# Four V tiles to a PSUM bank, gathers without staged row numbers, and U low parts ahead of the routing

## What is computed

```
q  = (h @ w_q) -> [t, 8 heads, 2, 128];  s = q . sub_keys (128 keys a half)
s1,i1 = top_k(s[:,:,0], 16);  s2,i2 = top_k(s[:,:,1], 16)
top_s,pos = top_k(s1 + s2 over all 256 pairs, 16);  idx = i1*128 + i2 at pos;  gate = softmax(top_s)
act = gelu(einsum('td,tkd->tk', x, u[idx]))          # 8*16 = 128 experts a token
out = einsum('tk,tkd->td', gate * act, v[idx])       # u, v: 16384 experts x 2048
```

## Time and profile before

| | us |
|---|---|
| median of 3 runs | 5671.56 (5666.36 to 5677.82) |
| the profiled execution | 5670.56 |
| its span, first to last instruction | 5668.8 |
| TensorE busy | 5059.5 (89%) |
| VectorE busy | 3760.8 (66%) |
| ScalarE busy | 1407.4 (25%) |
| GpSimd busy | 2950.0 (52%) |

### The profile page before, as it was taken

The page is one execution under the profiler, slowest core; times in us unless marked ns, Lnnn a source line. Parts: engine busy times, 40 slices in busy tenths (PEclk is TensorE's granted clock), DMA queues, the critical chain, the costliest instruction groups (busy, mean ns, idle before and its releaser), DMA issues. The chain is left out here.

```text
span 5668.8 us, 72848 instructions
## 1 busy us (share of the span) xinstructions
PE 5059.5 (89%) x25836; PEld 4495.4 (79%) x25836; DVE 3760.8 (66%) x5187; ACT 1407.4 (25%) x1138; POOL 2950.0 (52%) x1263
## 2 busy tenths in 40 slices
PE   6999979999998999999799899988997888888887
PEld 5877757777776787877599899988897888878786
DVE  3566658888887001001388799954327999999998
ACT  2223322222222222112232344422221111111111
POOL 2333323333332443443344555589986777777774
PEclk7999989999998999999899999999998999999999
DMA  1222212121212333333233577777777666666664
GB/s 72 89 89 82 88 54 72 63 78 66 77 65 80 113 111 135 119 119 142 95 117 113 198 266 262 257 272 272 279 271 264 237 229 252 239 242 236 228 249 152
DMA packets 214502, 913.24 MB, mean 161 GB/s; under 512 B 18352, under 2 KB 100912, under 8 KB 119856
## 3 DMA queue, kind: packets, MB, share of 16 engines
q1 hardware_dynamic: 177584, 644.12, 32.4%
q0 software_dynamic: 36864, 268.45, 12.7%
HBM read 837.00 MB, written 75.50 MB: 161 GB/s over the span
## 5 line engine op out<-in xcount | busy, mean ns | idle before, releaser
L149 POOL TENSOR_TENSOR ring_low<-ring_raw,ring_high 128x2048 fp32r<-128x2048 f32 x337 | 1618.8, 4804 | 1977.1 <-ACT ring_high L144 1953.6
L167 PE MATMUL rt_acc<-h_high,ring_high 128*128 128x384 f32 (+1 forms) x2304 | 799.7, 347 | 68.0 <-POOL ring_low L149 67.6
L168 PE MATMUL rt_acc<-h_low,ring_high 128*128 128x384 f32 (+1 forms) x2304 | 790.1, 343 | 0.0
L169 PE MATMUL rt_acc<-h_high,ring_low 128*128 128x384 f32 (+1 forms) x2304 | 789.7, 343 | 0.0
L144 ACT ACTIVATE ring_high<-ring_raw 128x2048 fp32r<-128x2048 f32 x337 | 645.1, 1914 | 390.4 <-PE out_acc L169 125.1
L1703 DVE CUSTOM_DVE_ANT_0 sb_rt_rows<-sb_rt_rows,sb_rt_h_tok 128x2048 f32<-128x2048 f32 x128 | 328.7, 2568 | 335.0 <-DMA sb_rt_rows<-u_rows,sb_rt_staged 332.2
L1885 DVE TENSOR_TENSOR x_mid_back<-x_mid_back,op_out 128x384 f32<-128x384 f32 x1024 | 491.5, 543 | 36.3 <-DVE sb_op_w_low L1872 16.7
L167 PEld LDWEIGHTS rt_acc<-h_high,ring_high 128*128 128x128 f32 x2304 | 436.7, 190 | 89.8 <-issue 39.8
L1836 PE MATMUL op_out<-sb_op_w_high,ring_high 128*128 128x384 f32 x1024 | 353.8, 345 | 134.9 <-DVE x_mid_back L1885 110.9
L167 PE MATMUL hg_acc<-h_high,ring_high 128*128 128x512 f32 x1024 | 432.8, 423 | 45.6 <-POOL ring_low L149 36.4
L1859 DVE SCALAR_TENSOR_TENSOR sb_op_total<-sb_op_rows,own_weight,sb_op_total 128x2048 f32<-128x2048 f32 x128 | 468.4, 3659 | 0.2
(11 more groups left out here) (298 smaller groups left out, 10758.3 us busy)
## 6 DMA issues: line engine op xcount, KB each, us to landing
ring_raw<-u_tiles SPq DMA_DIRECT2D x128, 1024.0 KB
ring_raw<-v_tiles SPq DMA_DIRECT2D x128, 1024.0 KB
ring_raw<-w_hg SPq DMA_DIRECT2D x64, 1024.0 KB
ring_raw<-w_ssd SPq DMA_DIRECT2D x48, 1024.0 KB
ring_raw<-w_mix_s SPq DMA_DIRECT2D x32, 1024.0 KB
ring_raw<-w_mix_h SPq DMA_DIRECT2D x32, 1024.0 KB
gelu<-sb_rt_gelu SPq DMA_DIRECT2D x128, 192.0 KB
gates<-sb_rt_table SPq DMA_DIRECT2D x12, 2048.0 KB, 7.3
```

Source lines behind the costliest of these rows:

```text
L149: nc.gpsimd.tensor_tensor(ring.low[:, slot], ring.raw[:, slot], ring.high[:, slot].bitcast(F32), ALU.subtract).then_inc(ring.low_ready, 1)
L167: nc.tensor.matmul(out, high[:, m], x_high[:, k, tokens], start=(k == 0), stop=False, skip_group_check=True)
L168: nc.tensor.matmul(out, high[:, m], x_low[:, k, tokens], start=False, stop=False, skip_group_check=True)
L169: last = nc.tensor.matmul(out, low[:, m], x_high[:, k, tokens], start=False, stop=(k == KT - 1), skip_group_check=True)
```

## The change

Three things. (1) `output_stage` sums four V tiles in a PSUM bank instead of two: a V load is now half of the columns (1024) of two tiles (`half_pair`), again 1 MB; of four tiles the left halves are two loads and give output tiles 0 to 7, then the right halves give 8 to 15. Each bank takes 12 matmuls, and there are 16 adds for four tiles. Weights are made for four tiles at once, in two buffers. (2) `gather` takes its row numbers straight from `row_of` at a fixed column; the two copies and `Staged` go, and GpSimd's loops with gathers are written out. (3) In `route_stage` GpSimd makes four more low parts before it waits for `own_ready`, and the gathers are spread by `FETCHED`: two on each of the first four tiles after, one a tile to the 48th, then 76 on 60 tiles.

```diff
 def load_tile(sp, ring, slot, tile, n):
     sp.wait_ge(ring.low_ready, ring.base + n - 1)
-    sp.dma_start(ring.raw[:, slot], tile).then_inc(ring.landed[slot], 16)
+    into = ring.raw[:, slot]
+    if len(tile.shape) == 3:
+        into = into.rearrange("p (a d) -> p a d", a=2)
+    sp.dma_start(into, tile).then_inc(ring.landed[slot], 16)
+
+def half_pair(tiles, first, half):
+    return tiles[first, :, half * (D // 2):(half + 1) * (D // 2)].rearrange("a p d -> p a d")
...
-def gather(nc, pool, rows, table, row_of, k, slot, staged):
-    nc.gpsimd.tensor_copy(staged.ap[0:OWN, slot:slot + 1], row_of[0:OWN, ds(k, 1)]).then_inc(staged.done, 1)
-    pool.wait_ge(staged.done, k + 1)
-    nc.gpsimd.tensor_copy(staged.seen[0:OWN, ds(k, 1)], staged.ap[0:OWN, slot:slot + 1])
+def gather(pool, rows, table, row_of, k, slot):
     return pool.indirect_dma_start(rows[0:OWN, slot], None, table,
-                                   bass.IndirectOffsetOnAxis(ap=staged.ap[0:OWN, slot:slot + 1], axis=0))
+                                   bass.IndirectOffsetOnAxis(ap=row_of[0:OWN, k:k + 1], axis=0))
...
+        GATE_TILES = 2 * GATE_PAIRS
+        LATE = KEYS - BEFORE - 2 * FREE_PAIRS - GATE_TILES
+        def FETCHED(i):
+            if i <= GATE_TILES:
+                return i + min(i, SLOTS)
+            return GATE_TILES + SLOTS + (HK - GATE_TILES - SLOTS) * (i - GATE_TILES) // LATE
...
-            split_low_all(nc, pool, ring, FIRST)
+            split_low_all(nc, pool, ring, FIRST + 2 * FREE_PAIRS)
             pool.wait_ge(own_ready, 1)
-            with pool.Fori(0, EARLY) as i:
-                two_pairs(i, 0, FIRST)
...
+            tiles = 2 * PAIRS - 2 * FREE_PAIRS
+            for i in range(tiles):
+                n = FIRST + 2 * FREE_PAIRS + 1 + i
+                split_low(nc, pool, ring, n % 2, n)
+                for k in range(FETCHED(i), FETCHED(i + 1)):
+                    fetch(k)
...
 # output_stage
+            for k in range(HK):
+                if k < HK - 1:
+                    low(k + 1, (k + 1) % 4)
+                fetch(k)
...
+            def group(g, buf):
+                pe.wait_ge(w_ready, g + 1)
+                for half in range(2):
+                    pe.wait_ge(ring.low_ready, ring.base + 4 * g + (2 * half + 2))
+                    for d in range(OUTS):
+                        pe.wait_ge(out_added, 2 * OUTS * g + (OUTS * half + d + 1))
+                        o = ps_out[d][:, 0:REST]
+                        for j in range(GROUP):
+                            s = 2 * half + j // 2
+                            m = slice(j % 2 * (D // 2) + d * P, j % 2 * (D // 2) + (d + 1) * P)
+                            nc.tensor.matmul(o, v_high[s][:, m], w_high[:, buf, j], start=(j == 0), stop=False)
+                            nc.tensor.matmul(o, v_high[s][:, m], w_low[:, buf, j], start=False, stop=False)
+                            last = nc.tensor.matmul(o, v_low[s][:, m], w_high[:, buf, j], start=False,
+                                                    stop=(j == GROUP - 1))
+                        last.then_inc(out_done if d < OUTS - 1 else half_done, 1)
...
+            def add_outputs(g, half):
+                for d in range(OUTS):
+                    if d % 4 == 2:
+                        s = 2 * half + d // 4
+                        add_rows(4 * g + s, s, g)
...
+            def group(g, buf, following):
+                add_outputs(g, 0)
+                if following:
+                    dve.wait_ge(w_ready, g + 1)
+                    weights(g + 1, 1 - buf)
+                add_outputs(g, 1)
```

More of the change, by code:

```diff
@@ L1794, in low @@
                                         ALU.subtract).then_inc(ring.low_ready, 1)
[L1796 to L1807, removed]
@@ L1808, in _, with fetch, high @@
-            body(N // 2 - 1, True)
+            def fetch(k):
+                pool.wait_ge(summed, k + 1)
+                gather(pool, rows, dram["v_rows"], row_of, k, k % 4).then_inc(gathered[k % 4], 16)
+            for k in range(HK):
+                if k < HK - 1:
+                    low(k + 1, (k + 1) % 4)
+                fetch(k)
         @block.scalar
         def _(act):
-            def high(g2, s):
-                act.wait_ge(ring.landed[s % 2], 32 * g2 + (8 * ring.base + 16 * (s // 2) + 16))
+            def high(g, s):
+                act.wait_ge(ring.landed[s % 2], 32 * g + (8 * ring.base + 16 * (s // 2) + 16))
@@ L1822, in _ @@
             for s in (1, 2, 3):
-                high(N // 2 - 1, s)
+                high(N - 1, s)
         @block.tensor
         def _(pe):
-            nc.tensor.nop().then_inc(pair_done, 2)
-            with pe.Fori(0, N // 2) as g2:
[L1829 to L1840, removed]
@@ L1843, in _ @@
+            with pe.Fori(0, N // 2) as g2:
+                for buf in range(2):
+                    group(2 * g2 + buf, buf)
+            pe.wait_ge(out_added, 2 * OUTS * N + OUTS)
             pe.wait_ge(summed, HK + 4)
@@ L1860, in add_rows, with weights @@
                                          ALU.mult, ALU.add).then_inc(summed, 1)
[L1862 to L1868, removed]
+            def weights(g, buf):
+                dve.wait_ge(in_landed, 32 * g + 32)
+                vec.tensor_tensor(*(a.rearrange("p j (b t) -> p j b t", t=GT) for a in (w[:], gelu[:])),
+                                  gate[:].rearrange("p b j t -> p j b t"), ALU.mult).then_inc(weighted, 1)
@@ L1869, in weights @@
                 dve.wait_ge(weighted, g + 1)
-                vec.tensor_copy(w_high[:, two], w[:]).then_inc(w_split, 1)
+                vec.tensor_copy(w_high[:, buf], w[:]).then_inc(w_split, 1)
                 dve.wait_ge(w_split, g + 1)
[L1872 to L1881, removed]
-                    else:
-                        dve.wait_ge(pair_done, g + 3)
-                    x = x_mid[:, d, OWN:T]
-                    vec.tensor_tensor(x, x, ps_out[d % OUTS][:, 0:REST], ALU.add).then_inc(out_added, 1)
+                vec.tensor_tensor(w_low[:, buf], w[:], w_high[:, buf].bitcast(F32), ALU.subtract).then_inc(w_ready, 1)
@@ new lines, in add_outputs @@
+            def add_outputs(g, half):
[3 more added lines that the diff above has]
+                        add_rows(4 * g + s, s, g)
+                    if d < OUTS - 1:
+                        dve.wait_ge(out_done, 2 * (OUTS - 1) * g + ((OUTS - 1) * half + d + 1))
+                    else:
+                        dve.wait_ge(half_done, 2 * g + (half + 3))
+                    x = x_mid[:, OUTS * half + d, OWN:T]
+                    vec.tensor_tensor(x, x, ps_out[d][:, 0:REST], ALU.add).then_inc(out_added, 1)
@@ L1887, in _ @@
+            def group(g, buf, following):
[4 more added lines that the diff above has]
+                add_outputs(g, 1)
             weights(0, 0)
-            weights(0, 1)
             dve.wait_ge(x_landed, 16)
             with dve.Fori(0, N // 2 - 1) as g2:
[L1891 to L1895, removed]
+                for buf in range(2):
+                    group(2 * g2 + buf, buf, True)
```

70 lines of the change are left out of this document (29 added, 41 removed).

## The result

The changed kernel takes 5413.33 us (median of 4, 5408.18 to 5417.11) against 5672.6 before (median of 4); the ratio is 0.9543, 95% interval 0.9526 to 0.9559. Forecast were 5459 us, with a range from 5360 to 5565.

The account below looks back on a forecast made before the run. VectorE was taken to bound the output stage, GpSimd the routing stretch from 3720 to 4040 us. 5670.6 - 178 (V tiles) - 38 (routing) + 3 (low parts) = 5458, with 1 us for the median 5459; range 5360 to 5565.

Parts of the forecast that it names:

- the 17 us wait: End of routing: TensorE's 17.36 us wait at 3149 for a low part would remain, with ScalarE's Exp in front.
- L1857's mean: Output stage, VectorE's row sums (L1859 before the change): mean would stay at 3.7 us or above.
- the longer issue: Gather instruction L1323 would take longer than 1.2 us, 0.98 undisturbed, as waiting for VectorE falls on it.
- V tiles four to a bank, with the gathers: Output stage: four tiles fall from 41.75 to 36.0 us, -178 us in all (ends -262 and -31).
- The copies cost nothing in the output stage: Output stage: removing two copies, some 0.9 us a gather, counted as nothing because GpSimd isn't the bound by its sum.
- the port account: Output stage: GpSimd holds the port 18.5 us, 3.2 pass beneath adds, 15.3 is waiting; four tiles 37.4 us.
- The rule on tensor_tensor and descriptor writing: By the skill, gathers never wait for VectorE sums: 0.6 us or more less each; the prediction's trace spoke against it.
- Routing: Routing stage, 32 tiles: lighter gathers, 16 tiles with two keeping 2.3 us each; -38 us (ends 0 and -65).
- Low parts past the routing: End of routing: four more low parts gain 0.7 us, first gathers' delay costs 3 us; +3 (ends -1 and +8).
- Clock in the output stage: Rival: short stalls keep TensorE at 1.2 GHz in the output stage; at 40% of groups 5784 us; chance 0.04.
- the saturated port: Rival: in the output stage VectorE waits out every low part, 40.6 us for four tiles, kernel 5621; chance 0.14.
- one cause: Output stage: VectorE's waiting came only from GpSimd's L1793 never running together with VectorE instructions with two SBUF operands.

Follow-up runs that it names:

- two_lows_on_vector: The changed kernel with two of every four low parts of the output stage made by VectorE instead of GpSimd: 5410.17 us, 0.9539.
- bank_alone: The kernel before with only the V tiles summed four to a bank; gathers with two copies, GpSimd's loops and routing as before: 5542.89 us, 0.9771.
- spread_alone: The kernel before with only the routing stage's new order (low parts four tiles past the routing, gathers by FETCHED), both copies kept: 5653.75 us, 0.9965.
- exp_later: The changed kernel with ScalarE's wait for exp_in and its Exp behind the high parts of tiles 33 and 34: 5388.23 us, 0.9497.
- no_gathers_out: The changed kernel without issuing the gathers of V rows in the output stage, sums over zero rows kept: 5382.57 us, 0.9485.
- low_on_vector: The changed kernel with the low part of every fourth V load made by VectorE instead of GpSimd: 5379.63 us, 0.9486.
- copies_alone: The kernel before with only the row-number copies gone and GpSimd's loops written out, two V tiles a bank: 5710.67 us, 1.0058.

## Why the prediction was right, and where it was off

The time lies inside the stated range, but 7 us below the forecast's own range (5420 to 5510), and the gain was 259 us for 213. Of the signs named, the 17 us wait, L1857's mean (3.86 us) and the longer issue (2.6 us) came true; the stage (1128.7 us for 1155 to 1165) and the tiles after the gates (8.5 us for 8.9) came out faster.

*V tiles four to a bank, with the gathers: -178 forecast, -210 measured.* The account of own work and waits holds: VectorE's own is 21.0 us (16 adds 7.4, four row sums 9.1, weights 1.76 + 0.96 + 1.76), the waits 4 x 1.52 + 3.4 + 0.1 + 4.4 = 14.0 (1.76 is the low part's undisturbed time in two_lows_on_vector, and taken for the mult, which takes 1.75 where nothing holds it in bank_alone), in sum 35.0 for 35.06. Forecast were 22.1 and 13.9. So the mis-sized term is own work: the weights were right (4.5), but the 1.0 us of loop gaps isn't there.

*The copies cost nothing in the output stage.* This step failed, though the sum hid it. Without them, the same V side takes 1128.7 us; with them, and with GpSimd's loops, 1207.7: 79 us for 128 gathers. So the V side alone was worth -131 where -178 was forecast, and the copies -79 where nothing was. That 36.0 came so near is in part luck: it was chosen between 34.2 and 37.4, and 37.4, the port account worked out with no gain for the copies, is what bank_alone shows (37.5). The error was to cost an edit on GpSimd by whether GpSimd has slack. Its idle time was inside a chain that goes through VectorE, where 0.9 us of copies is part of the 8.65 us turn. In the kernel before, the same edit costs 82 us instead. The prediction's "nothing" fits neither.

*The rule on tensor_tensor and descriptor writing.* In the changed kernel a gather's issue takes 2.8 us behind VectorE's row sum, and 2.59 beside the mult, a tensor_tensor with both inputs in SBUF, for 0.95 undisturbed. By what the Trainium skill ("SBUF — State Buffer", "Who interferes with whom") infers, it would not wait for the mult. The measurement decides: it does wait, as read from the earlier trace rows. By that rule the stage was to lie nearer to TensorE's own pace; it stands 1.3 us above it (35.06 for 33.76).

*Routing: -38 forecast, -57 measured.* The prices were of the right kind (16 doubles), but a double keeps 9/16 = 0.6 us, not 2.3. spread_alone shows what was left out: spacing the doubles gives 29 us even with copies. Of the 57, 46 are stalls that went (56 to 9 us); 10 are a term put at nothing, the clock: before, 97 matmuls of this stretch start more than 0.22 us after the one ahead without a stall, 12.4 us above the pitch of 0.1733 in all, and 2.7 after; the granted clock of the stretch went from 0.985 to 1.00.

*Low parts past the routing: +3 forecast, +4.5 measured.* ScalarE's exp_in did hold TensorE, shown by exp_later. Two waits were not foreseen: the first dot product takes 6.01 us, for 2.27, beside GpSimd's low part, and the cast of the row numbers waits.

*Clock in the output stage.* No loss: 1.00 (0.99 before).

Two slips in the sums change nothing: the low end of the V side is -264 by its own terms, not -262, and the saturated port's 5621 leaves out the +3 of the low parts.

## What to carry to other kernels

Where two engines exclude each other, write their program as one chain and count the turn (low part + sum + whatever stands between), since slack on the other engine is not free time. Move the shortest holder of the port into the turn, but only as much as the waits between the engines allow: the same subtraction took 4.6 us on GpSimd and 2.28 on VectorE, and one of four moved gained 34 us, two of four only 3. Test an edit in the kernel it is meant for: removing the copies was worth -79 us with four tiles a bank and +82 with two.

## What was not expected of the hardware

An instruction whose record starts within 0.1 us of the other engine's, even ahead of it (VectorE's 4823.74 to GpSimd's 4823.83, 4836.40 to 4836.50), can lose the port and wait all of the other's 4.6 us; start order in the records doesn't tell who gets it. In the changed kernel this locks into a rhythm: from the third group of four tiles to the last but one each takes 34.99 to 35.06 us. In bank_alone it alternates instead.

Instructions with a single SBUF operand wait too, which the prediction's "one cause" leaves out: the weights' cast takes 5.26 us on the mean in no_gathers_out and 0.96 in low_on_vector.

In copies_alone, with a stall of 6.4 us in each four tiles, the granted clock of the stage was 0.92; in the changed kernel, with 1.65 us, it was 1.00 once the first groups were through.
